# Second memory's products moved in half groups into the first attention's turns, all index logits ahead of them

## The reference, cut to what matters

```
h = rms_norm(x, norm_mix[0])
aq, ak, av, iq, ik, iw, bq, bk, bv = split(h @ ab_w_in)
# index logits: 8 index heads of 32, summed with a weight for each head
score[q, s] = sum_h iw[q, h] * relu(iq[q, h] . ik[s])      (causal)
sel = top 64 keys of score for each query
o_a = softmax over sel(aq . ak * 64**-0.5) @ av             8 heads, one shared key and value
o_b = causal softmax(bq . bk * 64**-0.5) @ bv               8 heads
x = x + concat(o_a, o_b) @ ab_w_out
k_l, v_l = split(rms_norm(mem, norm_mem_src[l]) @ mem_w_kv[l])    for both layers l = 0, 1
```

## Time and profile before

| | |
|---|---|
| median of 3 runs | 1381.91 us (1380.02 to 1382.62) |
| profiled execution | 1379.49 us, of which span 1377.8 |
| PE | 1299.9 us, 94% of the span |
| DVE | 996.5 us, 72% |
| ACT | 750.6 us, 54% |
| POOL | 184.7 us, 13% |
| PE in the chain that ended last | 85% |
| 129.56 to 160.97 us (the attention) | PE busy 22.91 of 31.41, DVE 24.42, ACT 23.51, POOL 17.15 |

### The profile page before, as it was taken

How to read it: one execution, slowest core, us unless ns; L and a number is a source line. 1 busy time by engine, 2 the same in 40 slices (tenths; PEclk the granted TensorE clock), 3 DMA queues, 4 the chain that set the end, 5 groups by cost and what they waited for, 6 DMA issues and landing times.

```text
span 1377.8 us, 18246 instructions
## 1 busy us (share of the span) xinstructions
PE 1299.9 (94%) x6687; PEld 1071.9 (78%) x6687; DVE 996.5 (72%) x1494; ACT 750.6 (54%) x951; POOL 184.7 (13%) x325
## 2 busy tenths in 40 slices
PE   6999898999999989989999999999879999999996
PEld 5876677888887877777888878787768888888885
DVE  5877776655555766666555558878688898989896
ACT  5654645444444358355444444484356776767674
POOL 0641301000000326020000000330134000000000
PEclk9999999999999989999999999999989999999999
DMA  8552133655656310335655555455659898989890
GB/s 279 176 170 87 62 122 122 215 184 191 191 166 183 117 44 2 107 109 170 223 184 183 183 176 178 159 182 185 247 186 372 313 353 324 368 309 371 308 361 32
DMA packets 122935, 271.85 MB, mean 197 GB/s; under 512 B 15191, under 2 KB 68589, under 8 KB 108269
## 3 DMA queue, kind: packets, MB, share of 16 engines
q1 hardware_dynamic: 122728, 270.84, 57.4%
q10 hardware_dynamic: 132, 0.03, 0.0%
HBM read 269.80 MB, written 1.05 MB: 197 GB/s over the span
## 4 chain that ended last, share of the span: by engine, by line
PE 85%; DVE 8%; ACT 3%; issue 2%; POOL 1%; DMA 0%; SPq 0%; DVEq 0%; ACTq 0%
PE bank L2380 25%; PE bank L2382 24%; PE bank L2381 24%; DVE t_wlo L1466 2%; PE bank L2864 1%; PE bank L2470 1%; PE bank L2482 1%; ACT t_whi L962 1%; PE bank L2447 1%; PE bank L2456 1%; PE bank L2502 1%; PE bank L2570 1%; PE bank L2537 1%; PE bank L2924 1%; PE bank L2689 1%
## 5 line engine op out<-in xcount | busy, mean ns | idle before, releaser
L1466 DVE TENSOR_TENSOR t_wlo<-t_raw,t_whi 128x2048 fp32r<-128x2048 f32 (+2 forms) x143 | 316.6, 2226 | 125.7 <-ACT t_whi L962 124.6
L2380 PE MATMUL bank<-t_whi,t_ahi 128*128 128x512 f32 (+3 forms) x808 | 317.1, 392 | 12.3 <-DVE t_wlo L1466 3.9
L2380 PE MATMUL bank<-t_whi,t_bhi 128*128 128x512 f32 (+1 forms) x800 | 311.1, 389 | 4.4 <-issue 4.1
L2381 PE MATMUL bank<-t_wlo,t_ahi 128*128 128x512 f32 (+3 forms) x808 | 312.0, 386 | 0.0
L2382 PE MATMUL bank<-t_whi,t_alo 128*128 128x512 f32 (+3 forms) x808 | 312.0, 386 | 0.0
L962 ACT ACTIVATE t_whi<-t_raw 128x2048 fp32r<-128x2048 f32 (+3 forms) x144 | 263.7, 1842 | 81.0 <-PE bank L2382 77.3
L2382 PE MATMUL bank<-t_whi,t_blo 128*128 128x512 f32 (+1 forms) x800 | 305.4, 382 | 0.0
L2381 PE MATMUL bank<-t_wlo,t_bhi 128*128 128x512 f32 (+1 forms) x800 | 304.8, 381 | 0.0
L2380 PEld LDWEIGHTS bank<-t_whi,t_ahi 128*128 128x128 f32 x808 | 152.5, 189 | 47.3 <-issue 7.1
L2380 PEld LDWEIGHTS bank<-t_whi,t_bhi 128*128 128x128 f32 x800 | 150.6, 188 | 35.2 <-issue 6.6
L2382 PEld LDWEIGHTS bank<-t_whi,t_alo 128*128 128x128 f32 x808 | 152.3, 188 | 30.2
(11 more groups left out here) (421 smaller groups left out, 1389.3 us busy)
## 6 DMA issues: line engine op xcount, KB each, us to landing
t_raw<-in_ffn_w_in SPq DMA_DIRECT2D x88, 512.0 KB, 4.6
t_raw<-in_ffn_w_out SPq DMA_DIRECT2D x22, 1024.0 KB, 4.9
t_raw<-in_w_in SPq DMA_DIRECT2D x18, 1024.0 KB, 5.1
t_raw<-in_exp_w_up SPq DMA_DIRECT2D x18, 1024.0 KB, 6.6
t_raw<-in_exp_w_gate SPq DMA_DIRECT2D x15, 1024.0 KB, 6.4
t_raw<-in_exp_w_down SPq DMA_DIRECT2D x15, 1024.0 KB, 6.7
t_memo<-in_exp_w_down SPq DMA_DIRECT2D x14, 1024.0 KB, 6.3
t_feat<-in_exp_w_gate SPq DMA_DIRECT2D x12, 1024.0 KB, 5.9
```

What stands on the lines that cost most here:

```text
L1466: dve.tensor_tensor(wlo[slot][:, 0:n], raw[slot][:, 0:n], whi[slot][:, 0:n].bitcast(F32), ALU.subtract).then_inc(lo_done, 1)
L2380: pe.matmul(dst, lhi, rhi_, start=start, stop=False)
L2381: pe.matmul(dst, lhi, rlo_, start=False, stop=False)
```

## The change

Four things are moved, on PE, ACT and DVE; SP and POOL keep their order.
The turns of the queries and keys go into the last group of the first key slab (`second_mem`, `dense_queries`) and ahead of the first two groups of the first value slab (`index_between`).
All 16 index logits go into the first value slab, two ahead of each group and two in its middle (`halfway`).
The second memory's two slabs are computed in half groups of 2 x 3 matmuls (`half_group`) inside PE's steps t = 0 to 8: 4, 4, 3, 4 and 1 of them, in `between` (behind the scores) and in the new `behind` (at the step's end). Their banks are emptied by `kv_out` in ACT's and DVE's loops, their units split there, and PE waits for the emptied banks in `outs_free` at t = 6 and 14.
DVE's passes 2 to 7 of the selection stand in its steps t = 0 to 7, and the half splits of the output product's first unit at t = 10 and 12. Since `ahi`, `alo` are still read up to t = 8, the heads of items 0 to 7 are split into `bhi`, `blo` (`head_rows`), and the output product reads its upper rows there (`upper`).

```diff
+        def head_rows(k, apart):
+            hi_, lo_ = (ahi, alo) if apart or k < 2 else (bhi, blo)
+            return hi_[:, bank_chunks(k, apart), :], lo_[:, bank_chunks(k, apart), :]
...
@@ ACT
+                    split_to(kv[0].end + 2)
+                    for b in range(4):
                         turn_copy(s["qturn"] + b, feat[:, 512 * b:512 * b + 512])
...
+                    kv_out(0)
+                    for b in (4, 5):
+                        turn_copy(s["qturn"] + b, feat[:, 512 * b:512 * b + 512])
+                    for i in range(4):
+                        relu(i)
+                    split_to(kv[1].end + 1)
+                    for b in (6, 7):
+                        turn_copy(s["qturn"] + b, feat[:, 512 * b:512 * b + 512])
+                    for i in range(4, 10):
+                        relu(i)
+                    split_to(kv[1].end + 2)
+                    for i in range(10, 16):
+                        relu(i)
+                    kv_out(1)
+
+                    def kv_between(t):
+                        if t in (0, 2):
+                            split_to(kv[2].end + 1 + t // 2)
+                        if t == 2:
+                            kv_out(2)
                         if t == 6:
                             split_to(kv[3].end + 1)
+                        if t == 8:
+                            kv_out(3)
...
@@ DVE
-                    for n in (1, 2):
-                        for v in range(2):
-                            split_to(kv[n].unit + v + RING)
...
-                    for t in range(1, 6):
-                        best_keys(t)
...
+                    split_to(kv[0].end + 2)
+                    kv_out(0)
+                    for i in range(4):
+                        logit(i)
+                    split_to(kv[1].end + 1)
+                    for i in range(4, 8):
+                        logit(i)
+                    best_keys(0)
+                    for i in range(8, 12):
+                        logit(i)
+                    best_keys(1)
+                    for i in range(12, 16):
+                        logit(i)
+                    split_to(kv[1].end + 2)
+                    def keys_ahead(t):
+                        if t == 0:
+                            best_keys(2)
+                            kv_out(1)
+                        if t in (2, 4):
+                            split_to(kv[2].end + t // 2)
+                    def keys_between(t):
+                        if t in (0, 2, 4):
+                            best_keys(3 + t // 2)
+                        if t == 2:
+                            kv_out(2)
+                        if t in (6, 7):
+                            best_keys(t)
+                        if t == 9:
+                            kv_out(3)
+                        if t in (10, 12):
+                            half_lo(t // 2 - 5)
...
@@ PE
+            def half_group(s, n, lhi, llo):
+                i, c, h = n // 4, n // 2 % 2, n % 2
+                if n == 0:
+                    banks_emptied(s)
+                if n % 4 == 0:
+                    unit_ready(s.unit + i)
+                slot = (s.unit + i) % RING
+                for k in (2 * h, 2 * h + 1):
+                    w = slice(s.width * k, s.width * k + s.width)
+                    ins = mm3(bank_of(s, c), lhi[:, 4 * i + k, P * c:P * c + P], llo[:, 4 * i + k, P * c:P * c + P],
+                              whi[slot][:, w], wlo[slot][:, w], 4 * i + k == 0, 4 * i + k == s.k - 1)
+                if n % 4 == 3:
+                    ins.then_inc(unit_used, 1)
...
-                    product(M[0]["kv"][1:2], bhi, blo, two_logits)
-                    pe.wait_ge(flag("qk_ready0"), 3)
-                    turns(s["qturn"] + 6, JOBS0[12:16], drain=False)
-                    product(M[1]["kv"][0:1], ahi, alo, two_logits, left=mem_turn[1])
-                    product(M[1]["kv"][1:2], ahi, alo)
...
+                    product(M[0]["kv"][1:2], bhi, blo, between=index_between, halfway=lambda group: two_logits(2 * group + 1))
                     emptied(s["qturn"] + 8)
+                    emptied(mem_turn[1] + 4)
+                    second_k, second_v = M[1]["kv"]
+                    def halves(t, first):
+                        slab, at_ = {0: (second_k, (0, 2, 4)), 2: (second_k, (4, 6, 8)), 4: (second_v, (0, 1, 3)),
+                                     6: (second_v, (3, 5, 7)), 8: (second_v, (7, 8, 8))}.get(t, (None, (0, 0, 0)))
+                        for n in range(at_[1 - first], at_[2 - first]):
+                            half_group(slab, n, ahi, alo)
+                    def outs_free(t):
+                        if t in (6, 14):
+                            slab = second_k if t == 6 else second_v
+                            pe.wait_ge(slab_act, slab.done_act)
+                            pe.wait_ge(slab_dve, slab.done_dve)
```

More of the change, by code:

```diff
@@ L1264, in _, with kv_out, relu @@
-                    product(kv[3:4], lambda s_, c: dsts[3][:, c, :], scale=mem_scale[:, 0:1], ahead=0)
-                    def first_out(t):
+                    def kv_out(n):
+                        act.wait_ge(unit_used, kv[n].end)
+                        act.activation(dsts[n][:, 0, :], bank_of(kv[n], 0), ACT.Copy, scale=mem_scale[:, 0:1]).then_inc(slab_act, 1)
+                    def relu(i):
+                        g, nk = s["index"] + i, P * (i // 8 + 1)
+                        act.wait_ge(scored, g + 1)
+                        if i >= 3:
+                            act.wait_ge(item_masked, g - 2)
+                        act.activation(relu_out[g % 3][:, 0:nk], SCB[g % 2][:, 0:nk], ACT.Relu).then_inc(exped, 1)
@@ L1272, in _ @@
+                    attention(items0(), s["heads"], (2, 3, 0, 1), between=kv_between)
                 else:
@@ new lines, in keys_between @@
+                    def keys_between(t):
[9 more added lines that the diff above has]
+                            half_lo(t // 2 - 5)
+                    attention(items0(), s["heads"], (2, 3, 0, 1), between=keys_between, ahead=keys_ahead)
@@ L2459, in turns, with attention @@
                     emptied(base + len(jobs) // 2)
-            def attention(items, run, between=None):
+            def attention(items, run, between=None, outs_free=None, behind=None):
                 n = run.n
@@ L2665, in banks_free, with index_between @@
[L2665 to L2671 removed]
+                    def index_between(group):
+                        if group == 0:
+                            pe.wait_ge(flag("qk_ready0"), 2)
+                            turns(s["qturn"] + 4, JOBS0[8:12], drain=False)
+                            emptied(s["qturn"] + 2)
+                        if group == 1:
+                            pe.wait_ge(flag("qk_ready0"), 3)
+                            turns(s["qturn"] + 6, JOBS0[12:16], drain=False)
+                        two_logits(2 * group)
@@ L2672, in _ @@
+                    def outs_free(t):
[3 more added lines that the diff above has]
+                            pe.wait_ge(slab_dve, slab.done_dve)
+                    attention(items0(), s["heads"], between=lambda t: halves(t, True), outs_free=outs_free,
+                              behind=lambda t: halves(t, False))
                 else:
```

112 lines of the change are left out of this document (44 added, 68 removed).

## The result

| | before | after |
|---|---|---|
| median | 1382.07 us (4 runs, 1380.02 to 1382.62) | 1373.72 us (4 runs, 1372.58 to 1374.46) |
| profiled execution | 1379.49, span 1377.8 | 1373.61, span 1371.9 |

The ratio is 0.9933, with a 95% interval of 0.9920 to 0.9945: 9.3 us less, or 7.6 to 11.1 by the interval; the two medians differ by 8.35. The forecast was faster, 1374.9 us within 1371.5 to 1379.5, and it held.

A forecast was written before the change was run, and what follows sets the result against it. PE bounds the kernel, 94% busy, idling in the attention's ring. Gains 1.9 ahead, 6.3 covered idle, less 1.2 switches, plus 0.35 behind T10, less 0.3 gaps: 7.1, taken as 7.0 from 1381.91, giving 1374.9 us, range 1371.5 to 1379.5.

The forecast's parts named there:

- (1): Ahead of the attention: it starts at 105.9 us, against 107.8 from the old start less the moved work; 1.9 us gained.
- (2): PE's work in attention steps T0 to T6: 27.7 us, so T8 starts at 133.7 and T10 4.4 later, at 138.1.
- (3): DVE's work in attention steps T0 to T6: 24.7 us, done near 134.0; masks for T10 ready at 135.6, against 138.1.
- covered idle time less switches: Attention T0 to T10: half groups cover 6.3 us of PE idle time, less 1.2 for switches between products and small matmuls.
- (5): From T10 to the output product: 15.8 us where it took 16.15, ending at 153.9; 0.35 gained.
- gaps: Allowance in the sum for small gaps: 0.3 us taken off the gain.
- slack of 2.5 us: DVE's masks of items 8 and 9 are done at 135.6, 2.5 us before T10's scores want them at 138.1.
- Rival A: DVE partly sets T0 to T8: T10 starts 3 us later, gain 4, 1378 us; chance 0.15.
- (4): Other new waits, for emptied memory banks, ACT's queue and loads: they cost nothing or are covered.
- The 1.4 us of returning clock: Behind T10: PE's return to full clock gives 1.4 us, 0.72 on the scores, the rest on turns and values.
- Rival B: DVE held by POOL's scaling in the attention, half splits held too: 2.8 us slower, 1384.7 us; chance 0.05.
- Rival C: Gain given back behind the attention to a later wait on a load or the clock: 1380 to 1384; chance 0.09.

The follow-up runs named there:

- the last experiment: Changed kernel with DVE's whole splits at T2 and T4 moved behind the step's reciprocals, beside GpSimd's multiplies: 1373.82 us.
- the kernel with the part ahead alone: Changed kernel with the second memory's slabs as whole products before the attention, selection passes 2 to 5 beside them, half splits put back: 1381.57 us, ratio 0.9992.
- the filled one: The kernel with the split at T6 plus unused transposes and matmuls in TensorE's two longest waits of each layer's attention over the memories: 1373.05 us, ratio 0.9922.
- the kernel with the split at T6: Changed kernel with the output product's first unit split whole at T6, no half splits at T10 and T12: 1373.60 us, ratio 0.9933, when first measured.

## Why the prediction was right, and where it was not

The sum was 7.1 us, taken as 7.0; the way measures 7.64 against the same trace. The main step held: the half groups fill PE's waits, and PE sets the pace to T10. The parts:

| step | predicted | measured, against the first trace of before |
|---|---|---|
| (1) ahead | 1.9 | 1.31 |
| (2), (3) T0 to T10: covered idle time less switches | 6.3 - 1.2 = 5.1 | 15.26 + 21.8 - 31.16 = 5.9 |
| (5) T10 to the output product | 0.35 | 16.15 - 15.66 = 0.49 |
| gaps | -0.3 | none |

**(1)** T0 came at 107.06, not 105.9. Of these 1.16 us, 0.55 is the profiled run's later start (64.53 and 63.98 for the first query matmul). The other 0.6 is the term that was too big. The prediction took a block of turns at 0.80 and the pairs of logits at 0.6 and 0.85. With its switches a block takes 0.89 to 0.96 here (83.84 to 86.09 and 86.09 to 88.35, less six matmuls of 0.2267; 88.35 to 89.31; 93.23 to 94.19), and a pair 0.65 or 0.85. The turns' place alone is 1.14, shown by its undoing. PE never waited for a logit, as said.

**(2)** right, 0.9 high: 27.11 for 27.7 and 4.05 for 4.4. The 31.16 us hold the 8.96 of before and 21.8 of half groups; that leaves 0.4 for switches, where the sum took 1.2.

**(3)** the step that was wrong in a size. Its slack of 2.5 us is 0.6. From T0 on, the prediction had T10 after 32.2 us and the masks done after 29.7. Measured are 31.16 and 30.55 (137.61 less 107.06). PE was 1.0 faster, so the same DVE work was wanted sooner, and DVE was 0.85 later: its masks began 2.25 behind PE (109.31) for the 1.9 allowed, it waited 2.85 us for item 2 where 1.5 was allowed, and its work to the end of the selection (136.37) was 24.2 for 24.7. The conclusion, PE sets the pace, held by 0.6 us. Rival A was that near.

**(4)** right: no new wait on PE ahead of T14.

**(5)** 15.66 for 15.8, but by luck: two errors nearly cancel. The 1.4 us of returning clock were no gain of the change: the second trace of before has 15.07 there. They were also too many. At full clock a wait of 0.41 for POOL stands where the slow rows stood (147.32), so the fall had cost 1.08. Against 15.07 the changed kernel is 0.6 slower in its tail: PE's waits there are 3.2 us in all, for 2.5 in the second trace, where the sum had 1.2 more. The wait at T14 was 1.52 for the predicted 1.2, those for POOL 0.74 for 1.1. Moving the split shows that they come of the half splits at T10 and T12.

**Rival B** had a true mechanism, shown by the last experiment, and a wrong place. In T0 to T8 the change puts DVE's splits ahead of the reciprocals on which POOL waits, so they don't meet there. At T10 they do: the half split beside POOL takes 1.55 us, the later one 1.20, and POOL's four multiplies at 141.24 take 2.88 for 1.90. Put beside each other at T2 and T4, they delayed a split by 0.4, far from 9.6.

**Rival C**, gain given back behind: the profile pair has 7.05 of lead at 160 to 480 us and 5.9 at the end, lost in stretches where the clock fell at other places. The medians differ by 8.35. Outside these stretches the lead keeps to 0.1 us. So no load absorbed it; what moves the lead is the clock.

**The reference time.** The prediction took 7.0 from the median although the profiled run of before lay 2.4 below it (2.6 below the later one of 1382.07). The medians put the gain at 8.35, 10.4 and 9.4 us, above what the way explains (6.57 or 7.64). Some 1 to 4 us of it are therefore outside the attention, and no term of the prediction has them; that the forecast still holds the median is in part luck. Their likely place is the clock: among 17 runs of before on one chip, those of mean clock 0.981 took 1383.5 to 1384.6 and the two of 0.984 and 0.985 took 1379.9 and 1379.8. Both traces of before are of executions near 1379.4. One of the other kind is on record in the kernel with the part ahead alone: 1383.56 us at 0.981, and from the output product on its instructions are those of before, but for the tiles that hold the first heads. Against the first trace of before it loses 4.6 us behind the attention, all at places where its clock is at 0.50 over more of the work: 1.6 near 200 us, 0.6 between 495 and 556, 1.6 near 950, 0.8 near 1014. The stretches near 200 and 950 in the trace of before, and below them the same work in that one:

```profile
209.79:212.53 2.74, 2.73 (x25) 2.74 (x25) 1.30 (x3) 0.89 (x4) 1.68 (x3) 1.00 0.00 0
950.47:954.00 3.53, 3.53 (x15) 2.92 (x16) 3.50 (x4) 0.09 (x1) 0.10 (x1) 1.00 0.64 85
```

```profile
209.29:213.66 4.37, 4.37 (x25) 4.37 (x25) 1.79 (x3) 0.88 (x4) 1.67 (x3) 0.61 0.00 0
952.16:957.30 5.14, 5.14 (x16) 4.09 (x16) 5.11 (x4) 0.08 (x1) 0.09 (x1) 0.67 0.73 149
```

So falls of the clock are what makes such an execution 4 us longer. That the changed kernel has fewer of them, and why, is argued from the mean clocks alone (0.984 in most of its runs, 0.981 to 0.983 in most of before); two of its own runs, at 0.983, took 1377.3.

## What to carry to other kernels

Work moved into a stage in which PE waits for a ring gains the idle time; dummy work there gained next to nothing here, so count what leaves the stage ahead. Check the slack of the engine behind it again with the faster PE, and test it by adding a known delay: it costs one run, and here it gave 0.6 us, as the trace did. Look for the helper's own waits (here 2.85 us on DVE) before placing its next job, and take a second trace before booking a half-clock stretch as a gain.

## What was not expected of the hardware

Two executions of one kernel agreed to 0.1 us over hundreds of microseconds and then stepped apart by 0.4 to 1.7 us at places where PE's granted clock was 0.50 in one and 1.00 in the other: at 147, 200, 490 to 560, 945 and 1003 us. Near 600 and 1003 us it fell in every trace but the filled one (600), not always over the same instructions. The falls lie in or behind waits of PE; that at 945 begins 1.3 us behind a wait of 2.01 us. In the kernel with the split at T6, this hid 1.84 us that each trace shows in the attention. What an execution gains or loses by such falls, up to 4.6 us behind the attention, is as large as what a careful reordering brings.
